# A two-block hybrid layer on one core: raw x is transposed as it lands, and its inverse roots are applied behind the latent projection

## The reference, cut to what matters

```
h = rms_norm(x, g_mix)            # x * rsqrt(mean(x*x) + eps) * g_mix, per token
proj = h @ w_in                   # q_mla, c_kv, k_rope, q_gla, k_gla, v_gla, a_gla, ...
kv = rms_norm(c_kv, g_ckv) @ w_ukv
k_pe = apply_rope(rms_norm(k_rope, g_k_rope))
log_a = log_sigmoid(a_gla @ w_gla_gate + b_gla_gate) / 16
kv_m = rms_norm(mem, g_mem) @ w_mem_kv
```

## Time and profile before

| | |
|---|---|
| time, median of 3 runs | 937.98 us (937.62 to 938.54) |
| the profiled execution | 936.98 us |
| its span | 934.5 us |
| PE busy | 922.6 us (99%) |
| VectorE busy | 700.7 us (75%) |
| ScalarE busy | 236.2 us (25%) |
| the chain that ended last, share of PE | 98% |

### The profile page before, as it was taken

The page is one execution under the profiler, slowest core; times in us unless marked ns, Lnnn a source line. Parts: engine busy times, 40 slices in busy tenths (PEclk is TensorE's granted clock), DMA queues, the critical chain, the costliest instruction groups (busy, mean ns, idle before and its releaser), DMA issues.

```text
span 934.5 us, 12482 instructions
## 1 busy us (share of the span) xinstructions
PE 922.6 (99%) x4968; PEld 582.1 (62%) x4968; DVE 700.7 (75%) x1212; ACT 236.2 (25%) x470; POOL 41.1 (4%) x65
## 2 busy tenths in 40 slices
PE   7999999999999999999999999999999999999998
PEld 5954455945555459999744459547864444469544
DVE  4875965589758687957899854888979799574676
ACT  5314422233333222332200011311203112323110
POOL 0400000000005400000000001000000000000000
PEclk9999999999999999999999999999999999999999
DMA  9753441453527524335455537532524334231721
GB/s 335 235 189 119 154 135 46 180 180 98 196 91 170 191 91 179 129 146 181 180 180 180 177 106 237 178 114 91 180 92 180 124 147 181 93 133 47 268 92 45
DMA packets 51066, 141.78 MB, mean 152 GB/s; under 512 B 4449, under 2 KB 8449, under 8 KB 50753
## 3 DMA queue, kind: packets, MB, share of 16 engines
q1 hardware_dynamic: 48128, 134.55, 41.1%
q0 software_dynamic: 2272, 5.84, 2.6%
q10 hardware_dynamic: 608, 0.61, 0.2%
HBM read 138.89 MB, written 2.10 MB: 151 GB/s over the span
## 4 chain that ended last, share of the span: by engine, by line
PE 98%; ACT 0%; DMA 0%; DVE 0%; issue 0%; DVEq 0%; ACTq 0%
PE pair L2244 31%; PE pair L2329 28%; PE pair L2325 16%; PE pair L2594 6%; PE turned L2185 4%; PE score L2594 3%; PE turned L2594 1%; PE score L2687 1%; PE score L2487 1%; PE score L2503 1%; PE score L2430 1%; PE score L2431 1%; PE score L2759 1%; PE turned L2674 0%; DMA ident<-in_c_ident 0%; PE score L2336 0%
## 5 line engine op out<-in xcount | busy, mean ns | idle before, releaser
L1158 DVE TENSOR_TENSOR arena<-arena 128x512 f32<-128x512 f32 (+5 forms) x345 | 192.2, 575 | 17.9 <-PE score L2594 4.1
L2244 PE MATMUL pair<-ring,hT 128*128 128x512 f32 (+2 forms) x448 | 186.2, 570 | 0.9 <-ACT hT L727 0.9
L2244 PEld LDWEIGHTS pair<-ring,hT 128*128 128x128 f32 x448 | 83.3, 190 | 88.6 <-issue 83.4
L2329 PE MATMUL pair<-ring,hT 128*128 128x512 f32 x208 | 94.3, 595 | 0.9 <-ACT arena L740 0.8
L2329 PE MATMUL pair<-ring,arena 128*128 128x512 f32 x208 | 93.2, 594 | 0.0
L2329 PE MATMUL pair<-arena 128*128 128x512 f32 x192 | 86.7, 593 | 0.0
L1158 DVE TENSOR_TENSOR arena<-pair,arena 128x512 f32<-128x512 f32 x63 | 44.3, 703 | 55.7 <-PE pair L2329 30.6
L1158 DVE TENSOR_TENSOR arena<-ring 128x2048 f32<-128x2048 f32 (+1 forms) x40 | 74.6, 1865 | 2.1 <-DMA ring<-in_w_ssm_out 0.8
L2244 PE MATMUL pair<-hT,ring 128*128 128x128 f32 (+1 forms) x448 | 72.6, 322 | 0.2 <-ACT hT L723 0.2
L2244 PEld LDWEIGHTS pair<-hT,ring 128*128 128x128 f32 x448 | 64.6, 191 | 6.8 <-ACT hT L723 1.0
L2329 PEld LDWEIGHTS pair<-ring,arena 128*128 128x128 f32 x208 | 38.5, 190 | 43.7 <-issue 43.5
(11 more groups left out here) (271 smaller groups left out, 1020.9 us busy)
## 6 DMA issues: line engine op xcount, KB each, us to landing
ring<-in_w_in SPq DMA_DIRECT2D x33, 2048.0 KB, 8.3
ring<-in_w_up SPq DMA_DIRECT2D x8, 2048.0 KB, 8.7
ring<-in_w_down SPq DMA_DIRECT2D x8, 2048.0 KB, 7.8
ring<-in_w_o SPq DMA_DIRECT2D x4, 2048.0 KB, 8.2
ring<-in_w_mem_kv SPq DMA_DIRECT2D x2, 2048.0 KB, 7.8
ring<-in_w_glu SPq DMA_DIRECT2D x2, 2048.0 KB, 8.1
ring<-in_w_ssm_out SPq DMA_DIRECT2D x2, 2048.0 KB, 7.7
ring<-in_w_ukv SPq DMA_DIRECT2D x1, 2048.0 KB, 9.0
```

The lines of the kernel that those rows point to most:

```text
L1158: return dve.tensor_tensor(o, a, b, op)
L2244: ins = pe.matmul(o_, s, m, start=a, stop=b)
L2329: ins = pe.matmul(h[bank_], rows[:, k, :], weights[:, k, :], start=not onto and k == 0, stop=k == 3, skip_group_check=True)
```

## The change

x is no longer scaled ahead of its transposes. Five things follow in the code:

- **Loads.** The latent's 320 columns come in two transfers of four blocks of channels each, the first between the two tiles of x, the second behind them. ScalarE issues all nine parameter rows, and behind them the forget gate's 16 columns; SyncE issues neither any more.
- **Warm-up.** The first ten matmuls and the three fillers run on a square of ones that VectorE writes, not on the identity.
- **Transposes.** PE transposes the raw tiles of x when they have landed. VectorE, not ScalarE, takes them out of PSUM: plain_turned multiplies four blocks at once by the gains of their channels into plain_x, which lies in gate_buf.
- **The latent** is the product of plain_x, without the roots. ScalarE applies the roots as the scale of the four operations that take it out of PSUM, when x_rows says that they are there.
- **The others.** VectorE writes each tile's inverse roots on the diagonal of a 128x128 square (scale_diag). PE multiplies ones by both diagonals, which puts the roots of 256 tokens in every row of a bank of PSUM (scale_rows); these two matmuls stand in the latent's second half, after two of its eight. VectorE multiplies plain_x by that bank into hT, one tile at a time (x_rows). On VectorE the first weight sum of g0 now stands ahead of its row sums.

```diff
@@ -350,6 +350,8 @@
         wgate = a1(512)
         junk = a1(1024)
         levels = a1(192)
+        plain_x = gate_buf.rearrange("p (k n) -> p k n", n=SEQ)
+        ones, diag = soft[:, 0:P], [soft[:, P * t + P:P * t + 2 * P] for t in range(TT)]
         adiag = a1(256)
         bgate = a1(1024)
         copied_q1, copied_q5, sum_z, sum_v = a1(512), junk[:, 0:512], across, junk[:, 512:1024]
@@ -507,12 +509,6 @@
 
         @block.sync
         def _(sp):
-            def rows_of(names):
-
-                for name in names:
-                    a, n = COLS[name]
-                    sp.dma_start(prow[a:a + n, :], d[name].rearrange("o (a b) -> (o a) b", b=P)).then_inc(sem("rows_in"), 16)
-
             def constants_of_rows():
 
                 sp.dma_start(inv[:, :], d["c_inv"]).then_inc(sem("consts_in"), 16)
@@ -528,9 +524,14 @@
                     src = d[name].rearrange("o a b -> o (a b)") if len(d[name].shape) == 3 else d[name]
                     sp.dma_start(gain[name], src.to_broadcast([P, w])).then_inc(sem("consts_in"), 16)
 
+            def latent(k0, k1, name):
+                dst = ring[:, 0, 0:KD * FIRST].rearrange("p (k n) -> p k n", n=FIRST)
+                src = d["w_in"][0, P * k0:P * k1, C_CKV:C_CKV + RANK + ROPE].rearrange("(k p) n -> p k n", p=P)
+                sp.dma_start(dst[:, k0:k1, 0:RANK + ROPE], src).then_inc(sem(name), 16)
+
             sp.dma_start(xres[:, 0, :], d["x"][0, 0:P, :]).then_inc(sem("x_in0"), 16)
+            latent(0, 4, "ckv_low")
             sp.dma_start(xres[:, 1, :], d["x"][0, P:2 * P, :]).then_inc(sem("x_in1"), 16)
-            rows_of(list(COLS)[4:])
             for n, j in enumerate(STREAMED):
                 name, _, w, r0, rows, c0, cols = JOBS[j]
                 slot = n % RING
@@ -550,8 +551,7 @@
                         sp.wait_ge(sem("half_done"), done(before, 1))
                 dst = ring[:, slot, 0:rows // P * cols].rearrange("p (k n) -> p k n", n=cols)
                 if name == "ckv":
-                    sp.dma_start(dst[:, :, 0:RANK + ROPE], d[w][0, :, c0:c0 + RANK + ROPE].rearrange("(k p) n -> p k n", p=P)).then_inc(sem(f"weights{slot}"), 16)
-                    sp.dma_start(dst[:, :, RANK + ROPE:FIRST], d[w][0, :, C_GA:C_GA + GR].rearrange("(k p) n -> p k n", p=P)).then_inc(sem("ga_in"), 16)
+                    latent(4, KD, "weights0")
                     continue
                 src = d[w][0, r0:r0 + rows, c0:c0 + cols].rearrange("(k p) n -> p k n", p=P)
                 sp.dma_start(dst, src).then_inc(sem(f"weights{slot}"), 16)
@@ -689,9 +689,10 @@
                     ins.then_inc(sem("turned_taken"), 1)
 
             act.dma_start(ident[:, :], d["c_ident"]).then_inc(sem("ident_in"), 16)
-            for name in list(COLS)[:4]:
-                a, n = COLS[name]
+            for name, (a, n) in COLS.items():
                 act.dma_start(prow[a:a + n, :], d[name].rearrange("o (a b) -> (o a) b", b=P)).then_inc(sem("rows_in"), 16)
+            act.dma_start(ring[:, 0, 0:KD * FIRST].rearrange("p (k n) -> p k n", n=FIRST)[:, :, RANK + ROPE:FIRST],
+                          d["w_in"][0, :, C_GA:C_GA + GR].rearrange("(k p) n -> p k n", p=P)).then_inc(sem("ga_in"), 16)
 
             def row_norm(t, src, lo, name, sink):
 
@@ -768,11 +769,9 @@
             for t in range(TT):
                 act.wait_ge(sem(f"x_in{t}"), 16)
                 row_norm(t, xres[:, t, :], 0, "x", junk)
-
-            turned(pcol[:, :], NCOLS)
-            act.wait_ge(sem("turned_taken"), 1)
-            for t in range(TT):
-                turned_rows(t, hT, "g_mix")
+                if t == 0:
+                    turned(pcol[:, :], NCOLS)
+            n_turn[0] += 4
             act.wait_ge(sem("mem_in"), 16)
             for t in range(TT):
                 row_norm(t, mem_tok[:, DM * t:DM * t + DM], 4, "mem", junk)
@@ -780,11 +779,14 @@
             ck = ckv.rearrange("p (t c) -> p t c", c=RANK + ROPE)
             for t in range(TT):
                 p = arrived("ckv", t)
-                act.activation(ck[:, t, :], p[:, 512 * t:512 * t + RANK + ROPE], ACT.Copy)
-                act.activation(a_tok[:, GR * t:GR * t + GR], p[:, 512 * t + RANK + ROPE:512 * t + FIRST], ACT.Copy)
-                act.activation(qdec[:, RANK * t:RANK * t + RANK], p[:, 512 * t:512 * t + RANK], ACT.Square, accum_out=st[:, 284 + t:285 + t])
+                act.wait_ge(sem("x_rows"), t + 1)
+                root = st[:, 1 + 2 * t:2 + 2 * t]
+                act.activation(ck[:, t, :], p[:, 512 * t:512 * t + RANK + ROPE], ACT.Copy, scale=root)
+                act.activation(a_tok[:, GR * t:GR * t + GR], p[:, 512 * t + RANK + ROPE:512 * t + FIRST], ACT.Copy, scale=root)
+                act.activation(qdec[:, RANK * t:RANK * t + RANK], p[:, 512 * t:512 * t + RANK], ACT.Square, scale=root,
+                               accum_out=st[:, 284 + t:285 + t])
                 ins = act.activation(kdec[:, ROPE * t:ROPE * t + ROPE], p[:, 512 * t + RANK:512 * t + RANK + ROPE], ACT.Square,
-                                     accum_out=st[:, 286 + t:287 + t])
+                                     scale=root, accum_out=st[:, 286 + t:287 + t])
             ins.then_inc(sem("taken_act"), 1)
             group_copy(0, 1)
             turned_rows(0, memT3, "g_mem")
@@ -1282,6 +1284,7 @@
                 mark(tt(c21, blocks(group(i)[0][4], c21), blocks(temporaries(i)[3], c21), ALU.subtract), "last_out")
 
             mark(dve.memset(st[:, 399:400], 1.0), "one_ready")
+            mark(dve.memset(ones, 1.0), "one_ready")
             def root_steps(a, scratch):
 
                 v, y, w = st[:, a:a + 1], st[:, a + 1:a + 2], st[:, scratch:scratch + 1]
@@ -1292,22 +1295,42 @@
                     yield dve.scalar_tensor_tensor(w, w, -0.5, v, ALU.mult, ALU.mult)
                     yield dve.scalar_tensor_tensor(y, w, 1.5, y, ALU.add, ALU.mult)
 
+            def plain_turned(t):
+
+                for g in range(2):
+                    n = 1 + 2 * t + g
+                    dve.wait_ge(sem("turned_ready"), n + 1)
+                    src = bank["turned"][n % 2][:, :].rearrange("p (k n) -> p k n", n=P)
+                    ins = tt(plain_x[:, 4 * g:4 * g + 4, P * t:P * t + P], src, bc(col("g_mix", 4 * g, 4).unsqueeze(2), [P, 4, P]), ALU.mult)
+                    ins.then_inc(sem("turned_taken"), 1)
+
+            def scale_diag(t):
+
+                mark(dve.tensor_scalar(diag[t], ident[:, :], st[:, 1 + 2 * t:2 + 2 * t], None, ALU.mult), "scale_diag")
+
+            dve.wait_ge(sem("turned_taken"), 1)
+            plain_turned(0)
             roots = [root_steps(0, 300), root_steps(2, 302)]
             dve.wait_ge(sem("x_ss"), 1)
             for _step in range(6):
                 link(next(roots[0]))
+            plain_turned(1)
             dve.wait_ge(sem("x_ss"), 2)
             for _step in range(5):
                 step(next(roots[0]))
                 link(next(roots[1]))
             own["x_s"] = 2
-            mark(dve.tensor_scalar(xn1[:, 0:DM], xres[:, 0, :], st[:, 1:2], None, ALU.mult), "x_rows")
+            scale_diag(0)
             for _step in range(6):
                 link(next(roots[1]))
-            mark(dve.tensor_scalar(xn1[:, DM:2 * DM], xres[:, 1, :], st[:, 3:4], None, ALU.mult), "x_rows")
+            scale_diag(1)
+            dve.wait_ge(sem("scale_rows"), 1)
             dve.wait_ge(sem("turned_taken"), 5)
+            for t in range(TT):
+                mark(tt(hT[:, :, P * t:P * t + P], plain_x[:, :, P * t:P * t + P],
+                        bc(bank["score"][1][:, P * t:P * t + P].unsqueeze(1), [P, KD, P]), ALU.mult), "x_rows")
+            group_t1(0)
             group_rows(0)
-            group_t1(0)
             for t in range(TT):
                 row_norm(t, mem_tok[:, DM * t:DM * t + DM], mem_tok[:, DM * t:DM * t + DM], 4, "mem")
             group_t3(0)
@@ -2212,6 +2235,8 @@
                     act_ = lambda k: yaT[:, SEQ * k:SEQ * k + SEQ]
                 else:
                     act_ = lambda k: hT[:, k, :]
+                if o == "ckv":
+                    act_ = lambda k: plain_x[:, k, :]
                 if o in SPLIT_TOKENS:
                     return [(p[:, SEQ * c + P * half:SEQ * c + P * half + P], ws[:, k, P * c:P * c + P],
                              by_residue(act_(k))[:, :, 32 * half:32 * half + 32], k == 0, k == nk - 1) for c in range(4) for k in range(nk)]
@@ -2230,7 +2255,7 @@
                 j = JOB[name]
                 o = JOBS[j][1]
                 if half == 0 and sub == 0:
-                    if JOBS[j][2]:
+                    if JOBS[j][2] and name != "ckv":
                         n = STREAMED.index(j)
                         pe.wait_ge(sem(f"weights{n % RING}"), 16 * (n // RING + 1))
                     i = OUTS.index(o)
@@ -2331,25 +2356,36 @@
                 if sub == of - 1:
                     ins.then_inc(sem("group_product"), 1)
 
+            x_rows = xres[:, :, :].rearrange("p t c -> p (t c)")
```

(32 more changed lines are left out.)

## The result

The changed kernel takes 942.49 us (median of 4 runs, 942.28 to 943.21) against 937.95 us (4 runs, 937.62 to 938.54): ratio 1.0049, interval 1.0032 to 1.0066. It is slower, by 4.5 us (0.5%). The profiled execution took 942.50 us with a span of 939.7, against 936.98 and 934.5.

The account below looks back on a forecast made before the run. The prediction took TensorE (PE), busy 99% of the span, as the bound. Moving the latent's start from 12.25 to 13.0, plus 1.3 and 1.35, gave +3.4 us: 941.4 us for the median, range 938.0 to 945.0.

Parts of the forecast that it names:

- 0.75 + 1.3 + 1.35: Delays in us forecast for the start of the latent, from there to group 0's first product, and beyond it.
- the prediction's own signs: Signs of being wrong: gate's weight before 9.6, no wait at the diagonals, or a wait not named.
- S: Start of the latent's first product on PE: 12.25 us before, forecast 13.0, the middle taken between 10.7 and 15.3.
- The gate's weight decides: Before the latent: the gate's weight, last on ScalarE's queue, lands last; chance 0.40 without a clock loss.
- Rival 2: PE idles from about 9.4 until the latent and its clock falls, costing up to 2.0 us; chance 0.18.
- One for one between the queues: In the start's loads, ScalarE's and SyncE's queues move packets about one for one, whatever their size.
- the first rival: Gate's weight lands early, the latent starts between 9.4 and 10.7, shift -0.2 to +1.1 us; chance 0.34.
- Tile 1 and g0's weights: Loads at the start: tile 1 lands at 8.1, so SyncE issues g0's first weights at 8.2 instead of 6.40.
- S to Q: Latent's start to group 0's first product: +1.3 us, with PE waiting 0.8 at the diagonals and two matmuls costing 0.45.
- From Q on: From group 0's first product: +1.35 us, VectorE's later chain stalling PE 0.25 at memory tile 0, 1.1 at product 4.
- Break-even at S = 9.6: The end moves by the latent's start minus 9.6 us, so only an earlier start than 9.6 gains.
- the fast rival: VectorE's lag costs PE nothing and the latent starts at 9.4: shift -2.4 us, 935.6; chance 0.08.

Follow-up runs that it names:

- after: The changed kernel itself, with raw x transposed and scaled later, against the kernel before: 942.49 us against 937.95, ratio 1.0049.
- fourth experiment: Changed kernel with the forget gate's weight back on SyncE's queue, behind the latent's second half: 941.74 us.
- third experiment: Changed kernel with 30 warm-up matmuls on ones instead of 10: 940.54 us.
- fifth experiment: Changed kernel with five of the nine parameter rows on SyncE right behind tile 0, the gate's weight still on ScalarE's queue: 944.19 us.
- sixth experiment: Changed kernel with both inverse roots and diagonals ahead of VectorE's gain product of tile 1: 940.78 us.
- first experiment: Changed kernel with VectorE's rotary angles behind group 0's last weight sum instead of ahead of it: 941.31 us.
- second experiment: Changed kernel with five of the nine parameter rows back on SyncE's queue, behind tile 1 of x: 941.90 us.
- eighth experiment: Changed kernel with five rows and gate's weight placed early on SyncE, 16 warm-ups, and diagonals, memory work, group 0's last weight sum and angles reordered: 937.03 us.
- ninth: The eighth experiment's kernel with group 0's last sums ahead of the rotary angles on VectorE: 935.33 us against 937.00 for the kernel before, ratio 0.9977.

## Why the prediction was right or wrong

The direction and nearly the size were right (941.4 forecast, 942.49 measured), but one large step was right by accident. The traces give 0.88 + 2.02 + 2.18 for the terms that were put at 0.75 + 1.3 + 1.35. By the prediction's own signs one counts against it: a wait that it had not named, the 4.60 for the rows.

- **S: 13.0 forecast, 13.13 measured, for another reason.** "The gate's weight decides" failed for after: it was issued at 4.58 and landed 6.9 later, at 11.5, while PE was still at slow transposes and fillers until 13.1. The fourth experiment shows that its queue did not matter there. In its place stood two things. First, the parameter rows: the prediction dated the column of gains by ScalarE's own work and gave the nine rows no landing of their own. It had read 2.7 us from issue to packets, for four rows of the kernel before; in after the last of nine took 5.49 to land, and the column was copied at 10.27 instead of 8.1. Second, the clock. The 13.0 itself was a choice of the middle between 10.7 and 15.3, so that it came out is luck.
- **Rival 2 happened, earlier than placed.** The prediction saw PE's idle time between 9.4 and S; it lay between the warm-up and the rows, 5.25 to 9.85. The prediction noted that the warm-up needs no DMA any more and so ends early, and priced that at nothing. That is the step that failed: a warm-up that ends 4.6 us before the work is no warm-up. Its price, by the third experiment, is 1.95 us, within the 2.0 given; its chance was put at 0.18, beside 0.40 for a late weight without it. The Trainium skill, TensorE: Matmul & The Clock Gate (Part 1), says that an idle PE falls back to the slow level; the trace agrees (0.50 after the wait of 4.60).
- **One for one between the queues** held in the fifth experiment (0.8 to 1.2 rows of q10 for a packet of q1), where q10 carried one transfer of 64 rows an engine. It gave S = 12.55 there with the gate's weight landing last, much as forecast, though the packets that it stood beside were those of tile 1 and the latent: g0's first weights were issued only at 10.77. In after it did not hold where it mattered. From 5 to 8 us q10 carried the parameter rows, transfers of one to eight rows of 512 B, and moved 73 packets to q1's 563 (the two lines below, the queues of after in that window): about one for eight. So the rows were late, and the gate's weight behind them began to move only at 8.1, not at 6.2 to 7.2. The Trainium skill, DMA: Bandwidth & Descriptors (Queues, rings and completion order), has an engine drain a whole packet, typically 9 to 17 descriptors, from one queue before it turns to the next. Both ratios fit that, if a transfer of a few rows gives its queue only a short turn; this is a reading, and no run tests it. By that rule the first rival does not follow either: the prediction counted the gate's weight in such turns (4 to 7), but did not count that SyncE's turns between them would be as long.

```profile
q1 hardware_dynamic: 563, 1.02, 101.1%
q10 hardware_dynamic: 73, 0.02, 3.1%
```

- **Tile 1 and g0's weights.** SyncE was to issue g0's first weights at 8.2; it did at 9.50. The turns of the small packets are not the reason, since q10 took 3.1% of the engines' time from 5 to 8 us (the lines above); it stays open.
- **S to Q: +1.3 forecast, +2.02 measured.** The wait at the diagonals (0.8 forecast, 0.61) and the two matmuls (0.45, 0.55) are right, and the sixth experiment removes the wait. Of the rest, 0.86, the first four products at the slow clock are 0.69 (3.22 against 2.53); the other 0.17 lies in the products around the wait. The two products of x with the roots took 2.48, as forecast (2 x 1.23).
- **From Q on: +1.35 forecast, +2.18 measured.** Mechanism right: VectorE has no gap from 22.03 to product 4, memory tile 0 waits 0.23 (forecast 0.25), and the first experiment takes the wait at product 4 away. The size is off: PE loses 1.64 there (45.23 + 3.57 for a product is 48.80, and product 4 begins at 50.44) against 1.1. The sum moved the old chain of VectorE as it was, but its angles grew from 3.61 us to 4.19, almost all of it in the first two operations (0.17 and 0.24 before). That is the 0.54. The two ran while GpSimd made two copies (the first line below, then VectorE's). In the second to sixth experiments the same copies also fall on the angles, which are 0.6 to 0.8 us longer each time; in the kernel before and in the first experiment they fall elsewhere, and the operations of the angles keep their old length. So VectorE, running late, met work of another engine that it used to miss. That the copies are the cause is not shown, since no run moves them alone.

```profile
39.69 1.60 POOL L593 COPY near<-arena 128x256 f32<-128x256 f32 x2 [3.44 <-DMA near<-in_c_masks]
40.24 0.49 DVE L1340 CAST posf<-posi 128x4 f32<-128x4 int32 x1
40.77 0.56 DVE L1343 TENSOR_SCALAR rope<-inv,posf 128x32 f32<-128x32 f32 x1
```

- **Break-even at S = 9.6.** This was for both lags left in place. No run has so early a start with both lags in place, so it is not tested. The eighth experiment, with S = 9.37 and these two lags taken out, gains 0.5 and the ninth 1.7, which fits a sum in which the early start alone is worth little.
- The rival of an early gate's weight is not what happened; the fast rival's condition, an early start with no VectorE lag, is what the ninth experiment builds: 1.7 under the kernel before, where 2.4 were forecast for that case.

## What to carry to other kernels

When work is brought forward to the landing of its input, list every load that it needs, small ones too, and give each the landing time it has beside the transfers that will then run, not alone. A warm-up must last until the first real work arrives; if a change lets it start earlier, it needs more of it. Work handed from an idle engine to a second busy one is a debt that shows tens of microseconds later, at the first place where the second engine had little slack.

## What the runs showed of the hardware

- Small rows of 512 B took 5.49 us from issue to landing beside large transfers on another queue, and 5.61 on the queue of the large transfers themselves (second experiment). Right behind tile 0 they were there by 6.1 (fifth), 3.6 us after the last was issued. Beside a full SyncE queue, transfers of a few rows got one packet through for about eight (73 to 563 in after), a transfer of 64 KB in rows of 64 B about one for one (fifth).
- A wait of 4.6 us cost more than its length: the clock fell in it, at 0.50 eight transposes took 1.97 instead of 1.09, and full speed came back only at 14.7 us, PE having resumed at 9.85. In the fifth experiment a wait of 4.51 had the same effect (first four products 4.82 against 2.47).
- The granted clock in a view of windows can read 1.00 ahead of the first change that the trace records: in 1.20:4.50 of after the 15 warm-up passes take 0.22 each, as in the stretch marked 0.50 (eight transposes in 1.97, against 1.09 at full speed). There the durations decide.
- While GpSimd made two copies of 128x256, two small operations of VectorE took 0.49 and 0.56 us instead of 0.17 and 0.24 (after).
